# The second product of an MLP as seven block products instead of eight, with the next hidden block interleaved

## The reference

```python
h2 = _rmsnorm(x, norm2_g[l])                       # 1024 x 1024
x = x + jnp.square(jax.nn.relu(h2 @ w_ff1[l])) @ w_ff2[l]   # w_ff1 1024 x 4096, w_ff2 4096 x 1024
```

## Time and profile before

| what | value |
|---|---|
| median of three runs | 2462.45 us |
| profiled execution, first to last instruction (span) | 2461.3 us |
| PE busy | 2383.1 us, 97% of the span |
| DVE, ACT, POOL busy | 1053.4, 616.5, 639.7 us |
| mean granted TensorE clock | 0.978 of full speed |

### The profile page before, as it was taken

How to read it: one execution, slowest core, us unless ns; L and a number is a source line. 1 busy time by engine, 2 the same in 40 slices (tenths; PEclk the granted TensorE clock), 3 DMA queues, 4 the chain that set the end, 5 groups by cost and what they waited for, 6 DMA issues and landing times.

```text
span 2461.3 us, 35407 instructions
## 1 busy us (share of the span) xinstructions
PE 2383.1 (97%) x12740; PEld 1996.1 (81%) x12740; DVE 1053.4 (43%) x1646; ACT 616.5 (25%) x1148; POOL 639.7 (26%) x481
## 2 busy tenths in 40 slices
PE   6999989989999999999979999899899999999999
PEld 6988878888888888888879888788888888888887
DVE  4048753363343333433440587433633334334333
ACT  4133432231212212112141333321322121121221
POOL 4245322221222212212132452321222122122220
PEclk9999989999999999999989999799999999999999
DMA  6222232211111111111142231322111111111111
GB/s 252 89 66 85 87 107 65 94 52 35 51 51 49 52 35 51 51 34 51 53 139 82 69 97 68 107 85 73 52 47 50 39 51 51 34 51 51 49 36 68
DMA packets 83357, 166.83 MB, mean 68 GB/s; under 512 B 18004, under 2 KB 45268, under 8 KB 83160
## 3 DMA queue, kind: packets, MB, share of 16 engines
q1 hardware_dynamic: 68056, 142.78, 17.6%
q10 hardware_dynamic: 15232, 23.16, 2.6%
HBM read 138.56 MB, written 31.54 MB: 69 GB/s over the span
## 4 chain that ended last, share of the span: by engine, by line
PE 93%; issue 2%; DVE 2%; ACT 1%; POOL 1%; ACTq 1%; DVEq 0%; SPq 0%; POOLq 0%
PE ps L878 85%; PE ps L974 1%; PE ps L1050 1%; PE ps L1044 1%; PE ps L1073 1%; PE ps L869 1%; PE ps L1074 1%; PE ps L1002 1%; DVE y L1180 1%; PE ps L989 1%; PE ps L1046 1%; PE ps L1081 0%; PE ps L964 0%; POOL wlo L770 0%; PE ps L1055 0%
## 5 line engine op out<-in xcount | busy, mean ns | idle before, releaser
L710 POOL TENSOR_TENSOR wlo<-raw,whi 128x1024 fp32r<-128x1024 f32 x152 | 368.4, 2441 | 1202.9 <-ACT whi L445 1202.6
L878 PE MATMUL ps<-hTh,whi 128*128 128x512 f32 (+1 forms) x1472 | 574.9, 391 | 0.0
L878 PE MATMUL ps<-hTl,whi 128*128 128x512 f32 (+1 forms) x1472 | 568.2, 386 | 0.0
L878 PE MATMUL ps<-hTh,wlo 128*128 128x512 f32 (+1 forms) x1472 | 565.9, 384 | 0.0
L1500 DVE TENSOR_TENSOR xs<-ps,xs 128x512 f32<-128x512 f32 x512 | 353.6, 691 | 319.2 <-PE ps L878 314.5
L878 PE MATMUL ps<-wlo,Uh 128*128 128x512 f32 x1024 | 405.4, 396 | 0.0
L878 PE MATMUL ps<-whi,Uh 128*128 128x512 f32 x1024 | 403.5, 394 | 0.0
L878 PE MATMUL ps<-whi,Ul 128*128 128x512 f32 x1024 | 403.2, 394 | 0.0
L678 ACT ACTIVATE rel<-ps 128x512 f32<-128x512 f32 x128 | 76.5, 597 | 1084.6 <-PE ps L878 1084.6
L878 PEld LDWEIGHTS ps<-hTh,wlo 128*128 128x128 f32 x1472 | 277.6, 189 | 62.0
L878 PEld LDWEIGHTS ps<-hTh,whi 128*128 128x128 f32 x1472 | 277.4, 188 | 61.0 <-issue 1.4
(11 more groups left out here) (168 smaller groups left out, 2572.3 us busy)
## 6 DMA issues: line engine op xcount, KB each, us to landing
raw<-in_wstream SPq DMA_DIRECT2D x168, 512.0 KB, 3.3
raw<-in_wtoken SPq DMA_DIRECT2D x20, 516.0 KB, 5.1
zD<-zst ACTq DMA_DIRECT2D x80, 129.0 KB, 1.8
xt<-out_y SPq DMA_DIRECT2D x16, 512.0 KB, 3.4
out_y<-xs SPq DMA_DIRECT2D x16, 512.0 KB, 2.6
zq<-zD SPq DMA_DIRECT2D x16, 320.0 KB, 2.8
xs<-in_x ACTq DMA_DIRECT2D x8, 512.0 KB, 10.9
out_y<-in_x ACTq DMA_DIRECT2D x8, 512.0 KB, 19.5
```

Of the source, the lines that this page charges most:

```text
L710: nc.gpsimd.tensor_tensor(lo_ap, raw[slot][:, 0:D], hi_ap.bitcast(F32), ALU.subtract).then_inc(w_lo, 1)
L878: mm = pe.matmul(out_ap, a, b, start=(c == 0), stop=(c == n - 1))
```

## The change

The second product of a half block (512 tokens x 256 hidden channels by 256 x 1024) is split in 2x2 blocks (256 tokens x 128 hidden channels by 128 x 512) and formed by seven block products with sums of blocks on either side, instead of eight. For this:

- PE: each product r is two token tiles by three matmuls of 512 columns, into two banks. Products 1, 3, 5 and 6 follow one another into banks 0 and 1, products 2 and 4 into banks 4 and 5, product 0 into banks 2 and 3; a product that follows adds to what stands in the banks (start is false from r = 3 on). After each product stand 6, 6, 6, 6, 6, 10 and 8 matmuls of the first product of the same half of the next chunk, into banks 6 and 7. A loop iteration is a chunk of two halves (b = 0, 1). The last chunk has no such matmuls between its products.
- DVE: after each product one add of 128x1024 to two tiles of xs (add). Four sums of 128x256 for each half (u_sums), two subtractions of 128x1024 and 128x768 for the lo parts (u_los), and four sums of 128x512 for each chunk's w_ff2 (w2_sums).
- ACT: relu and square of 128x512 in float32 (hidden), hi parts of the seven u blocks in two casts (u_his), hi parts of w_ff2's seven blocks of 128x512 (w2_hi), and of w_ff1's two units (w1_hi).
- POOL: lo parts of the seven blocks (w2_lo) and of the two units (w1_lo).
- Buffers: the ring is left out of the MLP; raw1, raw2, tS, w1h, w1l, w2h, w2l, uq, uS, uh, ul take its place. The constants ident, tri, gB and others move to a fixed place, and the selector is loaded anew in each layer.
- The output is written in two groups of four tiles, each after the last add of its half.
- Semaphores of two chains in the other phases are merged (a_del, a_scan, a_min to a_max; b_c1, b_c2, b_c3 to b_tap), with the same instructions and the same order.

```diff
 # PE
+                def product(p, b, r):
+                    base = l * (7 * HALVES) + (p * 14 + 7 * b)
+                    if r == 0:
+                        pe.wait_ge(u_lo, l * (2 * HALVES) + (p * 4 + (2 * b + 3)))
+                    if b == 0:
+                        pe.wait_ge(m2_lo, l * (7 * CH) + (p * 7 + (r + 1)))
+                    if r in (1, 3, 4, 5, 6):
+                        pe.wait_ge(f_acc, base + {1: 1, 3: 3, 4: 4, 5: 5, 6: 7}[r])
+                    for tp in range(2):
+                        us = slice(tp * P, (tp + 1) * P)
+                        h_, l_ = uh[b][:, U_AT[r], us], ul[b][:, U_AT[r], us]
+                        for j, (u, w) in enumerate(((h_, w2h), (h_, w2l), (l_, w2h))):
+                            mm = pe.matmul(ps[:, BANK[r] + tp, :], u, w[:, r, :], start=(r < 3 and j == 0), stop=(j == 2),
+                                           skip_group_check=True)
+                    mm.then_inc(f_y, 1)
+                FILL = (6, 6, 6, 6, 6, 10, 8)
+                def halves(p, more):
+                    for b in range(2):
+                        c = 0
+                        for r in range(7):
+                            product(p, b, r)
+                            if more:
+                                hidden_part(p + 1, b, c, FILL[r])
+                                c += FILL[r]
+                pe.wait_ge(f_rel, l * (2 * HALVES) + 4)
 # ACT, after the norm of the first chunk
+                for r in range(2, 7):
+                    w2_hi(0, r, True)
+                u_his(0, 0, True)
+                hidden_first(1, 0)
+                w1_hi(1, 0, False)
+                hidden_first(1, 1)
 # ACT, loop
+                    w1_hi(p + 1, 1, False); u_his(p, 1, False)
+                    hidden(p + 1, 0, 0, 6); hidden(p + 1, 0, 1, 7)
+                    w2_hi(p + 1, 0, False); w2_hi(p + 1, 1, False)
+                    u_his(p + 1, 0, False); w2_hi(p + 1, 2, False)
+                    hidden(p + 1, 1, 0, 6); w1_hi(p + 2, 0, False)
+                    for r in range(3, 7):
+                        w2_hi(p + 1, r, False)
+                    hidden(p + 1, 1, 1, 7)
 # POOL, loop
+                    w1_lo(p + 1, 1)
+                    for r in range(3):
+                        w2_lo(p + 1, r)
+                    w1_lo(p + 2, 0)
+                    for r in range(3, 7):
+                        w2_lo(p + 1, r)
 # DVE, loop
+                    add(p, 0, 0); u_sums(p, 1, 0); add(p, 0, 1); u_sums(p, 1, 1)
+                    add(p, 0, 2); add(p, 0, 3); u_los(p, 1, 0); add(p, 0, 4); u_los(p, 1, 1)
+                    add(p, 0, 5); add(p, 0, 6); w2_sums(p + 1, 0)
+                    add(p, 1, 0); w2_sums(p + 1, 1); u_sums(p + 1, 0, 0)
+                    add(p, 1, 1); u_sums(p + 1, 0, 1)
+                    add(p, 1, 2); add(p, 1, 3); u_los(p + 1, 0, 0); add(p, 1, 4)
+                    u_los(p + 1, 0, 1); add(p, 1, 5); add(p, 1, 6)
 # SP
+                for b in range(2):
+                    sp.wait_ge(f_acc, l * (7 * HALVES) + (7 * (HALVES - 1 + b) + 1))
+                    for t in range(4):
+                        sp.dma_start(out_t[b * 4 + t], xs[:, b * 4 + t, :]).then_inc(s_spill, 16)
...
```

More of the change, by code:

```diff
@@ L682, in split_f @@
[L682 to L697, removed]
+                    if t == 2:
+                        w2_hi(0, 0, True); w2_hi(0, 1, True)
@@ L1110, in hidden_quarter @@
                         mm.then_inc(f_u, 1)
[L1112 to L1134, removed]
-                            mm.then_inc(f_u, 1)
[L1136 to L1145, removed]
-                                             whi[(3 + a) % 4][:, n * 512:(n + 1) * 512], wlo[(3 + a) % 4][:, n * 512:(n + 1) * 512]) for a in range(2)])
-                            mm.then_inc(f_y, 1)
@@ new lines, in hidden_part @@
+                def hidden_part(p, b, c0, n):
+                    for c in range(c0, c0 + n):
+                        a, k, j = c // 24, (c % 24) // 3, c % 3
+                        if c % 24 == 0:
+                            pe.wait_ge(f_rel, l * (2 * HALVES) + (p * 4 + (2 * b + a - 1)))
+                            if b == 0:
+                                pe.wait_ge(m1_lo, l * HALVES + (p * 2 + (a + 1)))
+                        w = (w1h, w1h, w1l)[j][:, a, k * P:(k + 1) * P]
+                        x = (hTh, hTl, hTh)[j][:, k, b * 512:(b + 1) * 512]
+                        mm = pe.matmul(ps[:, 6 + a, :], w, x, start=(c % 24 == 0), stop=(c % 24 == 23))
+                        if c % 24 == 23:
+                            mm.then_inc(f_u, 1)
@@ new lines, in _, with halves @@
+                FILL = (6, 6, 6, 6, 6, 10, 8)
+                def halves(p, more):
+                    for b in range(2):
+                        c = 0
+                        for r in range(7):
+                            product(p, b, r)
+                            if more:
+                                hidden_part(p + 1, b, c, FILL[r])
+                                c += FILL[r]
+                pe.wait_ge(f_rel, l * (2 * HALVES) + 4)
+                alone(pe)
+                with pe.Fori(0, CH - 1) as p:
+                    halves(p, True)
@@ new lines, in _, with halves @@
+                w2_sums(0, 0); w2_sums(0, 1)
+                u_sums(0, 0, 0); u_sums(0, 0, 1)
+                u_los(0, 0, 0); u_los(0, 0, 1)
+                def halves(p, more):
+                    add(p, 0, 0)
+                    u_sums(p, 1, 0)
+                    add(p, 0, 1)
+                    u_sums(p, 1, 1)
+                    add(p, 0, 2); add(p, 0, 3)
+                    u_los(p, 1, 0)
+                    add(p, 0, 4)
+                    u_los(p, 1, 1)
+                    add(p, 0, 5); add(p, 0, 6)
+                    if more:
+                        w2_sums(p + 1, 0)
+                    add(p, 1, 0)
+                    if more:
+                        w2_sums(p + 1, 1)
+                        u_sums(p + 1, 0, 0)
+                    add(p, 1, 1)
+                    if more:
+                        u_sums(p + 1, 0, 1)
+                    add(p, 1, 2); add(p, 1, 3)
+                    if more:
+                        u_los(p + 1, 0, 0)
+                    add(p, 1, 4)
+                    if more:
+                        u_los(p + 1, 0, 1)
+                    add(p, 1, 5); add(p, 1, 6)
```

317 lines of the change are left out of this document (217 added, 100 removed).

## The result

The changed kernel takes 2406.55 us (2404.61 to 2407.71, four runs) against 2462.69 us for the one before in the same set of runs: a ratio of 0.977, 95% interval 0.9758 to 0.9782. It is 56.1 us faster where 29.4 were forecast. Later runs of the kernel before gave medians of 2462.9 to 2464.2.

The account below looks back on a forecast made before the run. PE was taken to bound the kernel, busy 97% of the span. Terms: -89.3 + 19.5 + 20.4 + 13 + 4 + 3 = -29.4 us on 2461.3, so 2433 us; own range 2420 to 2447, wide range 2400 to 2462.

Parts of the forecast that it names:

- rival 1: Loop and MLP starts: holding of DVE by POOL doesn't reach PE, giving 2402 us; chance 0.24.
- 384 matmuls at 0.2326, -89.3: MLP second product: 96 matmuls a chunk become 84, so 384 fewer at 0.2326 us each save 89.3 us.
- The pitch of the 48 hidden matmuls doesn't change: MLP loop: the first product's matmuls between the block products keep the earlier spacing, at no gain or cost.
- rival 5: Block products: longer pitch than the tiles', an exposed 0.17 us load at each giving back 76 us, 2509; chance 0.03.
- The loop's stall, +19.5: Half 1, before product 6: POOL holds u_los part 1, delaying add 5; 0.65 us in 30 iterations, 19.5 us.
- rival 3: Loop: POOL gets the port twice before u_los part 1, product 6 1.92 us late each iteration, 2471 us; chance 0.07.
- The starts, +20.4: Each MLP's start: PE waits 8.9 us for ACT's last relus, plus 1.3 at half clock; 20.4 us for both layers.
- The last chunks, +13: Each layer's last chunk: no fill, so PE waits for adds; 6.6 us a layer, 13 us (10 to 15).
- The ends, +4 and +3: Output writes after the last add: four tiles instead of one, +4 us at the end, +3 in layer 0.
- Nothing for the rest: Selector's reload, merged semaphores and moved buffers: no cost.
- Rival 4: Loop: PE's short stops each chunk lower the granted clock, +54 us once an iteration, 2487 us; chance 0.05.

Follow-up runs that it names:

- e6: Kernel before, work and order kept, its MLP weights in own tiles and Uh, Ul placed to agree with hTh and hTl modulo 256 bytes: 2428.5 us.
- e4: Changed kernel with w1h and w1l moved by 32 bytes and the tiles behind them by 128, uh1 and ul1 left in place: 2432.0 us.
- e1: Changed kernel with DVE's add of product 5 put ahead of u_los part 1 in half 1 of a loop iteration: 2383.6 us.
- e5: e1 with the start of each MLP reordered: u sums and casts first, last two relus ahead of most w2 casts, w1_lo before w2_lo: 2368.95 us.
- e8: e5 with the output written in pairs, tiles 0 and 1 of each half going behind the add of product 4: 2365.5 us.
- e9: e8 with add 5 put ahead of u_los part 1 in half 0 of each layer's last chunk: 2359.15 us.
- e3: Changed kernel with all 48 first-product matmuls of each half behind product 6, none between the products: 2895.3 us.
- e2: Kernel before with whi, wlo, Uh and Ul moved to agree with hTh and hTl modulo 128 bytes: 2454.4 us.
- e7: Changed kernel with w1h, w1l and the tiles behind them moved by 256 bytes, uh1 and ul1 left in place: 2406.0 us.

## Why the prediction was right, and where it was wrong

The direction was right, and the size was half of what came: -29.4 forecast, -55.4 between the spans. 2406.55 lies outside the forecast's own range, 2420 to 2447. It lies in the wide one, 2400 to 2462, only because that had been opened for rival 1's 2402, and rival 1's mechanism didn't come: holding reached PE in 28 of 30 iterations and at both starts, as forecast. So the wide range held by luck, through a term that the sum didn't have.

- **384 matmuls at 0.2326, -89.3.** The count was right. The step that failed is the one after it, "The pitch of the 48 hidden matmuls doesn't change" and the products' taken from the earlier trace rows. The matmuls that remain, 2784 a layer from the first product on, stand 0.2267 us apart: 2 x 2784 x 0.0059 = -32.9 us that the sum didn't have. I had asked only whether a pitch could get longer, by order of banks (rival 5), not by place in SBUF, though the diff moves each tile that PE reads in the MLP. By the kernels' allocation all of these are in step after it, while before it whi1, whi2 and Uh start 160, 192 and 160 bytes off hTh modulo 256. e6 shows this part alone, without the seven products, at -35.7. e4 loses most of it again (+25.5) with the work unchanged; that its 2432.0 is near the forecast's 2433 is chance.
- **The loop's stall, +19.5.** Right in place and mechanism, and 19.5 in the traces (e1), but partly by two errors that cancel. I had counted 30 stalls of 0.65. There are 28, since POOL has no w1_lo(p+2, 0) in a layer's last iteration, and each costs 0.70: an iteration takes 41.5 us and e1's 40.8. No run shows the 0.17 of a weight load that nothing hides; PE starts 0.06 behind the add, and the first matmul takes 0.34 instead of 0.23, the next few 0.23 to 0.24. No wait at product 3, none in half 0. That DVE and POOL alternate, and POOL doesn't come twice, was the point on which rival 3 hung, and it held.
- **The starts, +20.4.** The forecast's row for the clock was misread: between 498 and 506 PE wasn't idle throughout, but busy for 2.69 of 8 us. The term held even so: 8.0 us each against 8.9, and 1.8 against 1.3 for the clock (nine matmuls at 0.427 instead of 0.227): 19.7. The route was as forecast, DVE's sums and subtractions held in turn with POOL's in front of u_his, and e5 took most of it away by order alone.
- **The last chunks, +13.** From the first to the last matmul 26.5 and 26.4 us, against 83 x 0.2267 = 18.8: 15.2 together. The waits are four in each and not six. In e1, with the same waits and the clock at 1.00, it is 25.1, so 6.3 each against the 6.6 forecast; the half clock behind the wait of 2.38 us is the other 1.3. I had priced the clock at the starts and not here.
- **The ends, +4 and +3.** 4.1 and 4.3. e8 gave back 2.2 to 2.6 at each.
- **Nothing for the rest.** The other phases and the hidden quarters have 4.9 us more in this pair of traces. ident and gB moved among others, while hTh, woh and the ring kept their distances; but the same phases differ by up to 1.9 us between e5, e8 and e9 at the first transposes, so I leave that open.
- **Rival 4, the clock swinging in the loop,** did not hold: 1.00 throughout, with a wait of 0.4 us in 28 of 30 iterations. The Trainium skill (TensorE: Matmul & The Clock Gate, "A second HAM failure mode: psum-queue depth-cycling") says that brief idling between groups of matmuls makes the clock swing; that is seen in e3 alone, where the stops are longer (up to 3.4 us) and many, with a mean of 0.90.

The measured terms: -89.3 - 32.9 + 19.5 (28 x 0.70) + 19.7 + 15.2 + 8.4 + 4.9 = -54.5, against -55.4.

What the change is worth by itself: with all tiles in step, the order of before takes 2428.5 (e6) and the seven products 2406.6. By the spans, 2426.9 and 2405.9, that is 21 us. So some 21 us of the 56 are the seven products with their losses, and 35 are the tiles' places. Without the losses that e1, e5, e8 and e9 took away it is 69 of 105.

## What to carry to other kernels

When a diff moves the tiles that TensorE loads or streams, compare their addresses modulo 256 with those of before; a steady pitch above what the same form shows elsewhere is worth a run with the tiles moved. Saved matmuls need something independent between products that share a bank, and an add that releases a bank goes ahead of any DVE work that GpSimd can hold up. Where an engine's order makes TensorE wait for microseconds, price the clock behind it too, and look at it in each trace before a gain is put down to an edit: the same wait had half the clock behind it in some of these kernels and the full clock in another.

## What the runs showed of the hardware

- With the stationary and the streamed tiles in step modulo 256 bytes, fp32r matmuls of 512 columns ran at 226.7 ns (e1, e6). Out of step by 128 bytes they ran at 232 to 233 (e2's whi2, the output projection), in e4, by 32 and by 128, at some 231 to 233 on average, in a fixed order, and there took neighbours with them that are themselves in step (half 0's products). 256 bytes change nothing (e7). It was 35.7 us of 2464 in the kernel before (e6). Why places matter so isn't shown, and no tile was moved quite alone: e6 moved rel and ubf too.
- A DVE subtraction of 128x768 with both inputs in SBUF took 2.99 us for 0.95 behind a POOL subtraction of 128x1024, ending 0.82 us after POOL's. The Trainium skill (SBUF — State Buffer, "Who interferes with whom") has it that the second of the two to issue blocks until the first is done; the traces agree, in both directions, and two queued streams took turns at each start.
- A wait of 2.38 us in the last chunk, with two of 0.4 and 0.3 before it, had five to eight matmuls at 1.2 GHz behind it in five kernels (the changed one, e4, e5, e7, e8; both layers) and none in e1 (both layers). So the wait and its neighbours alone don't decide it. In e9 the wait was 1.5 us and the clock stayed up.
